# A gated convolution layer: the first two units projected from x without its norm for one half, and new orders on all engines

## The reference

```python
hn = rms_norm(x, norm_g)                      # x * rsqrt(mean(x*x) + 1e-6) * g
z = hn @ w_in                                 # 1024 x 3072
a, b, gate = jnp.split(z, 3, axis=-1)
u = a * jax.nn.sigmoid(b)
u = depthwise_causal_conv(u, conv_w, 31 taps) + conv_b
uf = (u - mu) * rsqrt(var + 1e-5) * ln_g + ln_b     # mu, var over the channels
u = jax.nn.silu(uf) * jax.nn.silu(gate)
return x + u @ w_out                          # 1024 x 1024
```

## Time and profile before

| | before |
|---|---|
| median of 3 runs | 423.15 us |
| the profiled execution's own time | 420.88 us |
| its span in the profile | 419.1 us |
| PE busy | 386.5 us (92%) |
| DVE busy | 326.3 us (78%) |
| POOL busy | 263.6 us (63%) |
| ACT busy | 199.5 us (48%) |

### The profile page before, as it was taken

The page is one execution under the profiler, slowest core; times in us unless marked ns, Lnnn a source line. Parts: engine busy times, 40 slices in busy tenths (PEclk is TensorE's granted clock), DMA queues, the critical chain, the costliest instruction groups (busy, mean ns, idle before and its releaser), DMA issues.

```text
span 419.1 us, 4665 instructions
## 1 busy us (share of the span) xinstructions
PE 386.5 (92%) x1680; PEld 308.4 (74%) x1680; DVE 326.3 (78%) x394; ACT 199.5 (48%) x259; POOL 263.6 (63%) x162
## 2 busy tenths in 40 slices
PE   1689999999999999999989999899958969999996
PEld 1367888888888888888868788688846747888885
DVE  1967999999999999999999379997877946561111
ACT  5567646521054756466356666544475522550000
POOL 2469999970269999999976999985467732000000
PEclk9999999999999999999999999999999998999999
DMA  8980131111111111011111101110021260048111
GB/s 314 401 306 2 50 101 52 50 50 52 50 52 50 50 52 50 0 52 50 51 52 50 50 8 45 52 50 0 2 91 59 102 250 0 2 144 306 52 51 50
DMA packets 11831, 34.06 MB, mean 81 GB/s; under 512 B 1312, under 2 KB 1568, under 8 KB 11808
## 3 DMA queue, kind: packets, MB, share of 16 engines
q1 hardware_dynamic: 11520, 33.56, 22.4%
q10 hardware_dynamic: 288, 0.21, 0.2%
HBM read 29.57 MB, written 4.19 MB: 81 GB/s over the span
## 4 chain that ended last, share of the span: by engine, by line
DVE 52%; PE 33%; issue 6%; ACT 3%; DMA 2%; POOL 2%; SPq 0%; POOLq 0%; DVEq 0%; ACTq 0%
DVE acc L740 37%; PE acc L417 12%; PE mm L381 10%; PE mm L417 7%; DVE dconv L716 2%; DVE u L692 2%; DVE acc L731 2%; DMA sgate<-x 2%; DVE dconv L740 2%; DVE stats L748 2%; PE mm L367 2%; ACT sgate L477 1%; DVE acc L729 1%; PE mm L411 1%; DVE nat L665 1%
## 5 line engine op out<-in xcount | busy, mean ns | idle before, releaser
L740 DVE SCALAR_TENSOR_TENSOR acc<-u,chan,acc 128x512 f32<-128x512 f32 (+1 forms) x213 | 200.0, 1015 | 1.5
L949 POOL TENSOR_TENSOR pconv<-pconv,prod 128x512 f32<-128x512 f32 (+1 forms) x90 | 156.0, 1733 | 14.9 <-ACT prod L519 5.2
L381 PE MATMUL mm<-x_hi,w_hi 128*128 128x512 f32 x352 | 140.4, 399 | 2.0 <-DVEq L695 2.0
L381 PE MATMUL mm<-x_hi,w_lo 128*128 128x512 f32 x352 | 139.5, 396 | 0.0
L381 PE MATMUL mm<-x_lo,w_hi 128*128 128x512 f32 x352 | 139.5, 396 | 0.0
L519 ACT ACTIVATE prod<-u,chan 128x512 f32<-128x512 f32 (+1 forms) x102 | 85.5, 877 | 28.4 <-POOL pconv L949 21.6
L381 PEld LDWEIGHTS mm<-x_hi,w_hi 128*128 128x128 f32 x352 | 66.3, 188 | 18.1 <-issue 2.4
L381 PEld LDWEIGHTS mm<-x_hi,w_lo 128*128 128x128 f32 x352 | 66.3, 188 | 16.1
L381 PEld LDWEIGHTS mm<-x_lo,w_hi 128*128 128x128 f32 x352 | 66.3, 188 | 15.7
L912 POOL TENSOR_TENSOR w_lo<-raw,w_hi 128x1024 fp32r<-128x1024 f32 x22 | 53.0, 2410 | 26.7 <-ACT w_hi L490 26.7
L490 ACT ACTIVATE w_hi<-raw 128x1024 fp32r<-128x1024 f32 x24 | 25.4, 1057 | 39.4 <-PE mm L381 37.9
(11 more groups left out here) (62 smaller groups left out, 423.5 us busy)
## 6 DMA issues: line engine op xcount, KB each, us to landing
raw<-w_in SPq DMA_DIRECT2D x24, 512.0 KB, 3.3
sgate<-x SPq DMA_DIRECT2D x8, 512.0 KB, 8.8
nat<-x_t SPq DMA_DIRECT2D x16, 256.0 KB, 10.8
raw<-w_out SPq DMA_DIRECT2D x8, 512.0 KB, 3.2
...
ident<-identity ACTq DMA_DIRECT2D x1, 64.0 KB, 5.1
```

What stands on the lines that cost most here:

```text
L381: ins = nc.tensor.matmul(bank(("unit", m, h)), w[:, m % 3, k, :], xx[:, k, h * HALF:(h + 1) * HALF], start=(k == 0 and i == 0), stop=(k == ...
L740: ins = nc.vector.scalar_tensor_tensor(dst, u_in(j, halves, k), w, running, ALU.mult, ALU.add)
L949: nc.gpsimd.tensor_tensor(dst, prod[:, (p - 1) % 3, width] if k == 1 else dst, prod[:, p % 3, width], ALU.add).then_inc(sums_done, 1)
```

## The change

- The x columns of half 1 come first. ACT and DVE split x times the gain, without the rms factor (`split_raw`), and PE projects half 1 of units 0 and 1 from that (`project_raw`).
- The missing factor is put on the products: DVE copies the b product out of PSUM (`copy_gate`), multiplies it by the rms row (`scale_gate`) ahead of the sigmoid, and multiplies the sigmoid by the same row ahead of the product with a (`conv_in_raw`). The norm of half 1 is made later for all other units, into the same buffers.
- The first weights are loaded and split in two pieces of 256 KB.
- Half 0 of units 0 and 1 is projected as a pair, and half 0 of units 2 and 3 comes ahead of their half 1 (`PASSES`).
- Tile 0 is convolved over both halves at once, on DVE and on POOL.
- All splits of x in half 0 and five of eight in half 1 are on DVE.
- The planner is gone: tables say how many steps, products, weight splits and transposes stand where. The norm's transposes in the last pass move from k 5 to k 3, and the stream has other counts of steps.

```diff
 
 TAPS0, TAPS1, TAPS6 = 9, 6, 16
-GPSIMD_PARTS = [(0, (0,), range(0, TAPS0)), (0, (1,), range(0, TAPS0)), (1, (0, 1), range(0, TAPS1)),
...
                 (3, (0, 1), range(0, 31)), (6, (0,), range(0, 31)), (6, (1,), range(0, TAPS6))]
-VECTOR_PARTS = [(0, (0,), range(TAPS0, 31)), (0, (1,), range(TAPS0, 31)), (1, (0, 1), range(TAPS1, 31)),
...
-LATE = [(7, 1), (6, 1)]
-
-
-UNIT_US, SPLIT_US, CONV_IN_US, STEP_US, SUM_US = 11.2, 0.0, 0.75, (0.67, 1.18), (1.25, 2.38)
...
-DELAYED = (0, 1, 2, 3, 4)
...
-
-LAG = 3
-LO_BY_POOL = (3, 5, 7)
...
-RSTD_TAP = 8
...
+                   (18, 1): [(3, 0)],
+                   (19, 1): [(3, 1), (5, 0)],
...
+
+STEPS_BY = [(0, 0, 0), (0, 0, 0), (2, 8, 8), (8, 9, 14), (17, 22, 25), (25, 25, 29), (33, 36, 36), (38, 45, 46),
...
+W_LO_AT = [0, 0, 0, 0, 0, 3, 5, 7, 16, 16, 16, 22, 26, 30, 31, 38, 40, 44, 48, 51, 63, 68, 75, 82]
+WO_LO_AT = [(0, 4), (1, 3), (2, 2), (3, 3)]
+
+
+LAG = 1
+LO_BY_POOL = ((), (0, 1, 5))
...
+ROWS_AT, SQUARE_AT = (2, 3, 4, 5), (-1, 1, 2, 3)
+SPREAD_AT = (6, 5)
+
+
+STEPS_MOMENTS = 0
+STEPS_NORM = (2, 6)
+RSTD_AT = 4
+NORM_AT = 3
+STREAM_STEPS = (0, 0, 3, 3, 3, 2, 3, 3, 2)
+STREAM_PRODUCTS = (0, 0, 2, 1, 0, 1, 0, 0, 0)
+WO_HI_AT = {1: 1, 2: 2, 4: 3, 6: 4, 7: 5}
 
...
 
 
-        JOBS = [("unit", 0, 0), ("unit", 1, 0), ("unit", 0, 1), ("unit", 1, 1)]
-        for m in range(2, NU):
-            JOBS += [("unit", m, 0), ("unit", m, 1)]
-            JOBS += [("conv", *jh) for jh in TRANSPOSE_AFTER.get(m, [])]
+        PASSES = [(0, 1), (1, 1), (0, 0), (1, 0), (2, 0), (3, 0), (2, 1), (3, 1)]
+        PASSES += [(m, h) for m in range(4, NU) for h in range(NH)]
+        JOBS = []
+        for m, h in PASSES:
...
-            return h == 1 or k in LO_BY_POOL
+            return k in LO_BY_POOL[h]
...
+
+                kind, j = UNITS[0]
+                cols = slice(part * KC * P // 2, (part + 1) * KC * P // 2)
+                sp.dma_start(raw[:, 0, cols], w_in[PART[kind], j, :, cols]).then_inc(done, 16)
+
+            load_first_weights(0, w0_in)
+            load_columns(1, 0)
+            load_first_weights(1, raw_in[0])
+            for k in range(1, KC):
+                load_columns(1, k)
+                if k == W1_AT:
+                    load_weights(1)
+            for t in range(TPH):
+                load_rows(t)
+            for k in range(KC):
+                load_columns(0, k)
+                if k in ROWS_AT:
+                    load_rows(TPH + ROWS_AT.index(k))
+            sp.wait_ge(w0lo_ready, 2)
+            load_weights(2)
+            for m in range(3, NU):
+                kind, j = UNITS[m]
...
+
+                if m:
+                    pe.wait_ge(wlo_ready, m)
+                for k in range(KC):
+                    if m == 0:
+                        if k == 0:
+                            pe.wait_ge(w0lo_ready, 1)
...
+                            pe.wait_ge(w0lo_ready, 2)
+                        pe.wait_ge(xlo_raw, k + 1)
+                    if (m, k) == (1, SPREAD_AT[0]):
+                        spread_rms(0)
+                    unit_terms(m, 1, k)
+
+            def project_pair():
+
                 for step in range(KC + LAG):
                     if step < KC:
-                        wait_lo(pe, h, step)
+                        wait_lo(pe, 0, step)
                     for m in range(2):
                         k = step - LAG * m
-                        if not 0 <= k < KC:
-                            continue
...
-                            pe.wait_ge(wlo_ready, m + 1)
-                        for i, (w, xx) in enumerate(terms(w_hi, w_lo, x_hi, x_lo)):
...
-                                                   start=(k == 0 and i == 0), stop=(k == KC - 1 and i == 2))
-                        if k == KC - 1:
-                            ins.then_inc(unit_ready[UNITS[m][0]], 1)
...
+                    if step == SPREAD_AT[1]:
                         spread_rms(1)
 
...
+
+                act.wait_ge(xt_in[1][k], 16)
+                nc.scalar.activation(x_hi[:, k, half(1)], nat[:, k, half(1)], ACT.Copy,
+                                     scale=norm_g[:, k:k + 1]).then_inc(xhi_raw, 1)
+
+            def split_first(part):
+
+                act.wait_ge(raw_in[0] if part else w0_in, 16)
+                ks = slice(part * KC // 2, (part + 1) * KC // 2)
+                cols = slice(part * KC * P // 2, (part + 1) * KC * P // 2)
+                nc.scalar.activation(w_hi[:, 0, ks, :].rearrange("p k n -> p (k n)"), raw[:, 0, cols],
+                                     ACT.Copy).then_inc(whi_ready if part else w0hi_ready, 1)
+
+            def sigmoid_scaled():
+
+                act.wait_ge(sig_scaled, 1)
+                nc.scalar.activation(sig[:, 1, :], sig[:, 1, :], ACT.Sigmoid).then_inc(sig_scaled, 1)
+
             def split_x(h, k):
 
                 act.wait_ge(hn_ready, KC * h + k + 1)
+                if h == 1:
+                    act.wait_ge(unit_ready["a"], 1)
...
                 if k == 0:
-                    act.wait_ge(u_ready, 1 if j == 0 and halves == (0,) else NH * (j + 1))
...
-                split_x(0, k)
-                if k == 1:
-                    split_w(1)
-                for i in range(TPH):
-                    if SQUARE_AT[i] == k:
-                        square(TPH + i)
+            for k in range(-1, KC):
+                if k >= 0:
+                    split_x(0, k)
...
+                    square(TPH + SQUARE_AT.index(k))
+            split_w(2)
+            sigmoid_scaled()
+            split_w(3)
+            read_unit(0, 0)
             for k in range(KC):
...
-
-            made = 0
-            for m in range(NU):
+
+            made, last_product = 0, len(PRODUCTS) - sum(STREAM_PRODUCTS)
+            for m in range(2, NU):
                 if m + 2 < NU:
                     split_w(m + 2)
...
-                quota = min(products_by[m], PRODUCT_END[6, 0] + RSTD_TAP + 3)
-                middle = (made + quota) // 2
-                while made < middle:
...
+
+                dve.wait_ge(xhi_raw, k + 1)
+                nc.vector.scalar_tensor_tensor(x_lo[:, k, half(1)], nat[:, k, half(1)], norm_g[:, k:k + 1],
+                                               x_hi[:, k, half(1)].bitcast(F32), ALU.mult,
+                                               ALU.subtract).then_inc(xlo_raw, 1)
...
+
...
+                ks = slice(part * KC // 2, (part + 1) * KC // 2)
+                cols = slice(part * KC * P // 2, (part + 1) * KC * P // 2)
+                nc.vector.tensor_tensor(w_lo[:, 0, ks, :].rearrange("p k n -> p (k n)"), raw[:, 0, cols],
+                                        w_hi[:, 0, ks, :].rearrange("p k n -> p (k n)").bitcast(F32),
+                                        ALU.subtract).then_inc(w0lo_ready, 1)
+
...
+
+                dve.wait_ge(unit_ready["b"], 1)
+                nc.vector.tensor_copy(sig[:, 1, :], bank(("unit", 0, 1))).then_inc(free(("unit", 0, 1)), 1)
+
+            def scale_gate():
+
+                dve.wait_ge(free(("unit", 0, 1)), 1)
+                dve.wait_ge(rms_all_ready, 2)
+                nc.vector.tensor_tensor(sig[:, 1, :], acc[:, 1, :], sig[:, 1, :], ALU.mult).then_inc(sig_scaled, 1)
+
+            def conv_in_raw():
+
+                dve.wait_ge(sig_scaled, 2)
+                nc.vector.tensor_tensor(sig[:, 1, :], acc[:, 1, :], sig[:, 1, :], ALU.mult).then_inc(sig_scaled, 1)
+                conv_in(1, 1)
 
...
 
                 _, j = UNITS[m]
-                dve.wait_ge(unit_ready["a"], NH * j + h + 1)
-                dve.wait_ge(sig_ready, NH * j + h + 1)
+                dve.wait_ge(unit_ready["a"], arrival(j, h))
+                if (j, h) == (0, 1):
...
                 if k == begin:
-                    dve.wait_ge(u_ready, 1 if j == 0 and halves == (0,) else NH * (j + 1))
...
+            for t in range(TPH):
+                rms_diagonal(t)
             make_hn(0, 0)
             for k in range(KC):
                 if k + 1 < KC:
                     make_hn(0, k + 1)
                 if not by_pool(0, k):
                     split_x(0, k)
...
+                    conv_in_raw()
+                if k > 0 and not by_pool(1, k - 1):
+                    split_x(1, k - 1)
+                if k == 5:
                     conv_in(1, 0)
+            if not by_pool(1, KC - 1):
+                split_x(1, KC - 1)
 
             total = len(STEPS)
-            done = 0
-            for m in range(NU):
-                quota = min(steps_by[m], total - STEPS_BEFORE_NORM - STEPS_AFTER_NORM - 13)
-                middle = (done + quota) // 2
-                if m == NU - 1:
-                    middle = quota = done + STEPS_BEFORE_MOMENTS
...
-                    moments(0)
-                    for _ in range(STEPS_BEFORE_NORM):
-                        step(done)
-                        done += 1
-                    normalise(0)
-                    for _ in range(STEPS_AFTER_NORM):
-                        step(done)
```

(20 more changed lines are left out.)

343 lines of the change are left out of this document (159 added, 184 removed), and 3 rows, old and new, of the table STEPS_BY.

## The result

The changed kernel took 410.38 us, the median of 4 runs, against 422.6 for the kernel before (421.88 to 423.35). One of the four, the profiled one, took 1334 us with a matmul only every 0.84 us; the other three took 409.03 to 410.91, with a median of 409.84, and are 0.970 of before, with a 95% interval of 0.966 to 0.974. That is 12.8 us less (12.2 by the median of all four); 11.5 were forecast. All experiments are compared with that set.

A forecast was written before the change was run, and what follows sets the result against it. PE and DVE share the bound, both paying for PE's late start. DVE's first step at 48 plus 238.8, 5.1 to the transposes and 35.6 of stream give 327.5 instead of 339: 423.15 - 11.5 = 411.6 us, range 405 to 418.

The forecast's parts named there:

- PE leading at the norm's transposes: Sign of being wrong: at the norm's transposes PE, not DVE, comes last; forecast had PE waiting about 4 us.
- a wait of PE for `conv_in` in the middle: Sign of being wrong: PE waits for PSUM banks mid-kernel; forecast had 3 to 5 us to spare.
- PE's first unit at 7.7, 96 matmuls at 36.9: Start of PE: begins 7.2 us earlier, and its first 96 matmuls end at 36.9 instead of 46.34.
- DVE's first step at 48 (45.5 to 53): Start of DVE: 11.5 us of work after 33.4, plus ACT and POOL delays, put its first convolution step at 48.
- 238.8 us from there to the end of the moments: DVE's stream of steps: 259.1 us before, less waits, full width, moved steps and one product, leaves 238.8.
- Transposes of the norm at 291.9, PE waiting 4 us for DVE: End of the middle: transposes start 5.1 us after the moments; PE alone would be there at 287.4.
- The stream, 35.6 (31 to 39): From the norm's transposes to the last convolution tile's transpose: 35.6 us, PE's own work 29.3.
- The rest, 80: After the stream, moments of half 1 and 12 output groups keep their order and take 80 us.
- more gain: Rival: POOL hardly meets the five subtractions, first step at 45.5, stream 33 us; 406.5 us, chance 0.17.
- The clock: Rival: PE stays at the lower clock through all 48 raw matmuls, 5.7 us more; 417.3 us, chance 0.18.
- The loads: Rival: half 0's pair waits for rows and columns, ends at 43, DVE starts at 55; 418.6, chance 0.09.
- Slower: Rival: work ahead of DVE's first step uses up the gain; first step at 62 gives 425.6; chance 0.06.

The follow-up runs named there:

- join_late: The changed kernel with the join of POOL's part of tile 0 four steps later on DVE; 407.98 us, 0.965 of before.
- raw_clear: The changed kernel with POOL's split of unit 1's weights held back until all raw x_lo subtractions are done; 409.46 us, 0.968 of before.
- rows_first: The changed kernel with the four row tiles of half 0 loaded ahead of the first weights and columns; 415.73 us, 0.981 of before.
- tile0_halves: The changed kernel with DVE's part of tile 0 in two passes of half width again; 409.16 us, 0.970 of before.
- pe_late: The changed kernel with twelve more matmuls on PE between the pair of half 0 and unit 2; 411.76 us, 0.975 of before.
- dve_late: The changed kernel with four memsets on DVE ahead of its first convolution step; 412.42 us, 0.975 of before.
- combined: The changed kernel with last w_out splits earlier, tile 0's join four steps later, three stream steps ahead of the moments, ACT's split_v before its copy; 401.91 us, 0.952 of before.

## Why the prediction was right, point by point

The difference was 1.3 us off (-12.8 for -11.5), and 0.3 between the two profiled executions (a span 11.8 us shorter). The core of the mechanism held: PE's earlier start is carried through to the end. That the number is so near is in part luck: behind it stand two errors of nearly 3 us that cancel, and two of the signs by which I would be wrong did show, PE leading at the norm's transposes and a wait of PE for `conv_in` in the middle.

- **PE's first unit at 7.7, 96 matmuls at 36.9.** Measured 7.10 and 36.78. The lower clock was taken at 8 us and was 3.1, which should have brought some 2 us. It brought nothing, since the next column was late by 1.76: the subtraction beside POOL, where I had said that neither DVE nor ACT holds PE. In join_late 12 matmuls came 0.43 us behind the one before, not 6, PE waited 0.70 and not 1.76, and the next one started at 14.78 all the same. I was right on the sum, with too slow a clock in place of a late column. raw_clear shows that POOL is what held the subtraction, and rows_first that a head start is worth all of itself.
- **DVE's first step at 48 (45.5 to 53).** Measured 46.62. The 11.5 us of work were right. ACT cost 0.8 (1 taken) and POOL 0.9 in place of 2: two of the five subtractions took 1.13, the other three the usual 0.69, and POOL's last x split had ended at 44.3. The Trainium skill's page "SBUF — State Buffer", section "Who interferes with whom", makes the order of issue decide who blocks. The trace agrees with that and shows the price: two subtractions paid 0.44 each, what was left of a POOL instruction already running, where a whole one for each of the five had been my upper bound.
- **238.8 us from there to the end of the moments.** Measured 283.75 - 46.62 = 237.1. The stalls of 13.4 us for PE went as forecast. The sentence that no queue order of POOL or ACT shows a need they can't meet did not hold: DVE waited 3.26 us for POOL at the join, and that wait swallowed the 2.9 of tile 0's full width (tile0_halves). I had looked at POOL's busy time, 206 of 257 us, where I should have asked when ACT's products can come. That the term came out 1.7 short all the same is luck. I had counted five steps as moved behind the moments; by the two traces they are eight, since the kernel before had 19 there and not 22 (5.3 us for 3.3). And the two joins with POOL's parts took 4.7 us before, one of them 3.22 at 121.29, and 2.5 now, which was in no sum. The moments thus ended just ahead of the 284 to 290 that I had given.
- **Transposes of the norm at 291.9, PE waiting 4 us for DVE.** Measured 289.10 and 0.23, and this step of the prediction failed: PE leads here, not DVE. ACT's part of the norm stands behind its reading of the last unit, which waits for PE, and DVE had been ready 1.1 us. PE without its wait for DVE is there at 288.03 (join_late; 287.4 forecast). DVE was forecast 3 us late: 1.4 at the first step, 1.7 in the stream of steps. pe_late shows PE's lead, all 2.8 us of it. dve_late shows that DVE's delay counts as well, since the two are tied by the banks: PE is late once DVE frees one late, at 95.41 there and by 1.05 us at 238.67 in the changed kernel, where I had seen 3 to 5 us to spare.
- **The stream, 35.6 (31 to 39).** Measured 38.44, the second error, of 2.8. The waits were right: 38.44 - 31.94 = 6.5 us against 35.6 - 29.3 = 6.3. The mis-sized term is PE's own work, 31.9 in place of 29.3. I had taken it over from the kernel before, where 6 unit matmuls stand behind the transposes; at k 3 they are 12, 1.4 us more. Eight matmuls behind the wait of 3.30 start 0.43 us apart, which is 1.6: I had priced waits at their length, though the earlier trace rows show that the clock fell behind one. combined has no wait over 1.66 here, the full clock, PE busy 30.66 and a stream of 35.77.
- **The rest, 80.** Measured 79.76.

Of the rivals, *more gain* had its first step (46.6 where it had 45.5) and not its stream of 33. *The clock* fell: it rose after 3.1 us, with the columns arriving one by one. *The loads* fell: the pair began at 23.79. *Slower* was 13 us away.
